# A two-block transformer kernel on one core: block 2's input projection and the query projection fed with unnormalised, turned residuals

## The reference, cut to what matters

```
x   = rms_norm(x2, norm_final)                      # end of the first block
h   = rms_norm(x, norm1_w) * (1 + scale1) + shift1  # scale, shift from silu(c) @ w_ada + b_ada
q, k, v, r, a_lr, su, sv, g_a, g_b = split(h @ w_in)
...                                                 # gated linear attention, spatial gating, merge
x   = x + gate1 * (merged @ w_out)                  # called x3 below
h2  = rms_norm(x, norm2_w) * (1 + scale2) + shift2
x   = x + gate2 * peer(h2)                          # queries h2 @ w_q, keys, top 16, experts
out = rms_norm(x, final_norm_w)
```

## Time and profile before

| what | value |
|---|---|
| median of 3 runs | 1415.91 us (1415.56 to 1416.72) |
| the profiled execution's own time | 1417.08 us |
| its span | 1415.3 us |
| granted TensorE clock, mean share of full | 0.988 |
| PE busy | 1371.8 us, 97% |
| POOL, DVE, ACT busy | 1055.6, 757.9, 710.4 us |

### The profile page before, as it was taken

One profiled execution on the slowest core, in us unless ns is written; L12 is line 12 of the kernel. 1 busy time (PEld: TensorE's weight loads), 2 busy tenths in 40 slices (PEclk: granted clock), 3 DMA queues, 4 the chain that ended last, 5 costly groups with the idle time before them and its releaser, 6 DMA issues.

```text
span 1415.3 us, 28961 instructions
## 1 busy us (share of the span) xinstructions
PE 1371.8 (97%) x9764; PEld 1220.6 (86%) x9764; DVE 757.9 (54%) x1617; ACT 710.4 (50%) x1133; POOL 1055.6 (75%) x469
## 2 busy tenths in 40 slices
PE   7998999999999998999999999999999999999997
PEld 7887899998877876999999999999977777878885
DVE  4655433335258526249991276666588788511113
ACT  6354555555355444435556533433455555556663
POOL 6654688886777985768888877777777777788885
PEclk9999999998999999999999999999999999999999
DMA  8453677763645456545555544444445444465552
GB/s 306 153 179 120 237 282 275 284 256 134 208 144 175 159 185 250 191 132 187 180 183 186 179 164 157 154 162 155 156 159 166 164 163 163 168 248 193 193 193 89
DMA packets 72651, 263.02 MB, mean 186 GB/s; under 512 B 8208, under 2 KB 9104, under 8 KB 72224
## 3 DMA queue, kind: packets, MB, share of 16 engines
q1 hardware_dynamic: 72608, 262.46, 53.9%
HBM read 259.81 MB, written 2.62 MB: 185 GB/s over the span
## 4 chain that ended last, share of the span: by engine, by line
PE 88%; DVE 6%; issue 2%; ACT 1%; DMA 1%; POOL 1%; SPq 0%; ACTq 0%; POOLq 0%; DVEq 0%
PE bank L865 14%; PE bank L883 14%; PE bank L866 14%; PE bank L867 14%; PE bank L884 13%; PE bank L885 13%; PE bank L1271 3%; DVE arena L1741 1%; POOL wlo L433 1%; DMA raw<-stream 1%; PE bank L983 1%; PE bank L1253 1%; DMA col<-cols 0%; PE bank L941 0%; DVE bank L1369 0%
## 5 line engine op out<-in xcount | busy, mean ns | idle before, releaser
L433 POOL TENSOR_TENSOR wlo<-raw,whi 128x1024 fp32r<-128x1024 f32 x432 | 1041.6, 2423 | 320.1 <-ACT whi L503 316.9
L503 ACT ACTIVATE whi<-raw 128x1024 fp32r<-128x1024 f32 x432 | 455.8, 1057 | 347.4 <-PE bank L885 256.9
L865 PE MATMUL bank<-xh,whi 128*128 128x256 f32 x1600 | 462.4, 289 | 4.2 <-DVE xl L1332 2.4
L866 PE MATMUL bank<-xl,whi 128*128 128x256 f32 x1600 | 455.4, 285 | 0.0
L867 PE MATMUL bank<-xh,wlo 128*128 128x256 f32 x1600 | 455.0, 284 | 0.0
L883 PE MATMUL bank<-whi,xh 128*128 128x512 f32 x800 | 321.6, 402 | 12.0 <-DVE xl L1939 4.1
L865 PEld LDWEIGHTS bank<-xh,whi 128*128 128x128 f32 x1600 | 309.8, 194 | 9.4 <-POOL wlo L433 3.7
L884 PE MATMUL bank<-wlo,xh 128*128 128x512 f32 x800 | 313.1, 391 | 0.0
L885 PE MATMUL bank<-whi,xl 128*128 128x512 f32 x800 | 312.9, 391 | 0.0
L866 PEld LDWEIGHTS bank<-xl,whi 128*128 128x128 f32 x1600 | 309.9, 194 | 1.2
L867 PEld LDWEIGHTS bank<-xh,wlo 128*128 128x128 f32 x1600 | 309.6, 193 | 0.0
(11 more groups left out here) (285 smaller groups left out, 1160.3 us busy)
## 6 DMA issues: line engine op xcount, KB each, us to landing
raw<-stream SPq DMA_DIRECT2D x432, 512.0 KB, 3.3
arena<-ada SPq DMA_DIRECT2D x48, 512.0 KB, 4.8
arena<-rows SPq DMA_DIRECT2D x5, 512.0 KB, 8.6
xs<-x SPq DMA_DIRECT2D x2, 512.0 KB, 6.0
arena<-rows SPq DMA_DIRECT2D x1, 1024.0 KB, 5.5
x_spill<-xs SPq DMA_DIRECT2D x1, 1024.0 KB, 6.1
xs<-x_spill SPq DMA_DIRECT2D x1, 1024.0 KB, 6.1
out<-arena SPq DMA_DIRECT2D x2, 512.0 KB, 2.6
```

The costliest lines, as they stand in the source:

```text
L433: nc.gpsimd.tensor_tensor(wlo[:, slot, :], raw[:, slot, :], whi[:, slot, :].bitcast(F32), ALU.subtract).then_inc(lo_done, 1)
L503: nc.scalar.activation(whi[:, slot, :], raw[:, slot, :], ACT.Copy).then_inc(hi_done, 1)
L865: nc.tensor.matmul(dst, h_, xh[:, k, :], start=(k == 0), stop=False)
L866: nc.tensor.matmul(dst, h_, xl[:, k, :], start=False, stop=False)
```

## The change

Both projections are fed from the raw residual: PE turns x2 (and x3) as soon as each 128x512 piece is there (`turn_of`), ACT and DVE apply only the gain (`upper_raw`, `turned_raw`), and the first tiles start without a norm. The activations get two more columns holding the shift (`xhs`, `xls`), so each of these f_tiles has 258 columns. The norm's root is turned into a row (`root_row`) after 3 (2) tiles, copied to `in2_r` (`wq_r`), and each tile's result is multiplied by the row and gets its own shift column added when it is read (`normed`, three DVE instructions in place of one). What follows needs the true h: DVE multiplies the turned banks by gain and row (`rowed`), ACT adds the shift (`shifted`), and at the end of the projection `xh` and `xl` are written anew (`upper_normed`, `turned_normed`). The two roots of block 2's input become one formula. `ada_columns` 3 to 7 move into the MLP, after 51 of its 64 tiles; the decays move into `m_sv`. `ada_row` 8 to 11 move between the projections' tiles, with new banks. SP's order changes with it: 12 tiles instead of 8 before block 2's constants, 16 instead of 8 query tiles before the spill, keys loaded before it. The last four tiles are done two banks at a time.

```diff
+            def turn_of(group, src, ready, tt, bs):
+                for b in bs:
+                    pe.wait_ge(S(ready), 2 * tt + b // 2 + 1)
...
+            def normed(n, d_, src, row, scale, done):
+
+                if n >= 2:
+                    v.wait_ge(S(done), n - 1)
+                wshift = wshifts[:, n % 2:n % 2 + 1]
+                own(nc.vector.tensor_copy(wshift, src[:, T:T + 1]))
+                own(ttt(d_, src[:, 0:T], row, ALU.mult)); own.sync()
+                if scale is None:
+                    tsc(d_, d_, wshift, None, ALU.add).then_inc(S(done), 1)
+                else:
+                    tsc(d_, d_, wshift, scale, ALU.add, ALU.mult).then_inc(S(done), 1)
...
+            def shift_lower(n, shifts):
+
+                v.wait_ge(S("shift_hi"), n)
+                ttt(xls[:, :, T:T + 2], shifts.unsqueeze(2).to_broadcast([P, KC, 2]), xhs[:, :, T:T + 2].bitcast(F32),
+                    ALU.subtract)
...
+                if i == N_FFN - 2:
+                    v.wait_ge(S("ada_cols"), 8)
+                    ttt(mod[:, :], bank[7][:, 0:32], c_("bada"), ALU.add).then_inc(S("mod_done"), 1)
...
+            def weighted(b):
+                v.wait_ge(S("x2_done"), b + 1)
+                ttt(xn[:, b // 2, (b % 2) * 512:(b % 2 + 1) * 512], x_half(b), tmp[:, (b % 2) * 512:(b % 2 + 1) * 512],
+                    ALU.mult).then_inc(S("x2_weighted"), 1)
...
+            shift_lower(SHIFTS["in2"], mod[:, 0:8])
+            weighted(0)
+            turned_raw("in2", gain_fin, (0, 1))
+            weighted(1)
+            turned_raw("in2", gain_fin, (2, 3))
+            weighted(2)
+            weighted(3)
...
+            for n in range(N_IN2_F):
                 v.wait_ge(tile_used, T_IN2_F + n + 1)
+                normed(n, qk[:, n, :], bank[IN2_BANK[n]], in2_r, 128 ** -0.5 if n < 4 else None, "qk_out")
+                if 2 <= n < 6:
+                    rowed("in2_T", gain_fin, in2_r, n - 2)
+                if n == 5:
+                    v.wait_ge(S("roots"), rooted("fin"))
+                    for tt in range(TT):
+                        stt(xres[:, tt, :], xres[:, tt, :], rs("fin", tt), tmp, ALU.mult, ALU.mult)\
+                            .then_inc(S("fin_done"), 1)
+                if n in (4, 6):
+                    gate_row(8 + (n - 4) // 2, gate1, "gate1_b").then_inc(S("gate1_done"), 1)
+            turned_normed("in2_T", "in2n")
...
+            def qk2_tile(n, turned=None, half=None):
+
+                pe.wait_ge(S("x2_done" if n < 3 else "qk_out"), n + 1 if n < 3 else n - 2)
+                f_tile((T_IN2_F + n) % R, T_IN2_F + n + 1, bank[IN2_BANK[n]][:, 0:T + 2], turned, xhs, xls, half)
+
+            for n in range(3):
+                qk2_tile(n, None if n else "in2")
+            pe.wait_ge(S("roots"), rooted("in2"))
+            pe.wait_ge(S("x2_done"), 4)
+            root_row("n1", bank[3], "in2_row")
+            qk2_tile(3)
+            pe.wait_ge(S("in2_row_out"), 1)
             ada_row(8)
+            qk2_tile(4)
+            qk2_tile(5)
+            pe.wait_ge(S("gate1_done"), 1)
             ada_row(9)
+            qk2_tile(6)
             pe.wait_ge(S("gate1_done"), 2)
+            qk2_tile(7, half="in2_half")
...
-            for b in range(4):
+            for banks in ((0, 1), (2, 3)):
                 for c in range(N_PEER - R, N_PEER):
-                    expert_m(c, None, final=(c == N_PEER - 1), banks=(b,), used=b == 3)
+                    expert_m(c, None, final=(c == N_PEER - 1), banks=banks, used=banks == (2, 3))
```

More of the change, by code:

```diff
@@ L394, in _ @@
                 ada_tile(n)
-            for n in range(T_WQ, T_WQ + 8):
+            for n in range(T_WQ, T_WQ + 16):
                 tile(n % R, n * P, n - R + 1)
@@ L867, in f_tile @@
                     last = nc.tensor.matmul(dst, l_, xh[:, k, :], start=False, stop=(k == KC - 1))
+                    if half and k == KC // 2 - 1:
+                        last.then_inc(S(half), 1)
                 last.then_inc(tile_used, 1)
@@ L1017, in ada_row @@
                 pe.wait_ge(ada_used, 4 * (g - g % 2 + 2))
-                nc.tensor.matmul(bank[6 + g % 2][:, :], one.to_broadcast([P, P]), ada_sum(g), start=True, stop=True)\
+                nc.tensor.matmul(bank[ROW_BANK[g]][:, :], one.to_broadcast([P, P]), ada_sum(g), start=True, stop=True)\
                     .then_inc(S("ada_rows"), 1)
@@ L1145, in _, with pairs @@
             transposes("mlp_T", "mlp", xres)
-            def pairs(base, count, group, name, name_of_turn):
+            LATE = 12
+            def pairs(base, count, group, name, name_of_turn, late):
                 def m_of(slot, count_, u, ready, **kw):
@@ L1175, in _ @@
-            for n in range(2, N_IN2_F):
-                pe.wait_ge(S("qk_out"), n - 1)
-                f_tile((T_IN2_F + n) % R, T_IN2_F + n + 1, bank[4 + n % 2][:, 0:T])
-            pe.wait_ge(S("gate1_done"), 2)
-            pe.wait_ge(S("xg_out"), 4)
-            pe.wait_ge(S("consts2_in"), 96)
-            for k in range(KC):
-                last = nc.tensor.matmul(bank[6][0:16, 0:T], wal[:, k, :], xg[:, k, :], start=(k == 0),
-                                        stop=(k == KC - 1))
@@ L1185, in _, with decays @@
-            last.then_inc(S("alr"), 1)
-            m_group(T_IN2_M, "m_sv")
+            qk2_tile(6)
+            pe.wait_ge(S("gate1_done"), 2)
+            qk2_tile(7, half="in2_half")
+            def decays(k):
+                if k != KC - 2:
+                    return
+                pe.wait_ge(S("xg_out"), 4)
+                pe.wait_ge(S("consts2_in"), 96)
+                for k in range(KC):
+                    last = nc.tensor.matmul(bank[6][0:16, 0:T], wal[:, k, :], xg[:, k, :], start=(k == 0),
+                                            stop=(k == KC - 1))
+                last.then_inc(S("alr"), 1)
@@ L1187, in _ @@
+            m_group(T_IN2_M, "m_sv", "in2n", before=decays)
             pe.wait_ge(S("alr_out"), 1)
```

336 lines of the change are left out of this document (201 added, 135 removed).

## The result

The changed kernel took 1436.88 us in the median of 4 runs (1436.01 to 1439.85), the one before 1416.32 beside it: a ratio of 1.0149, 95% interval 1.0133 to 1.0165. It is 1.5% slower, 8 us more than the 1428.9 of the forecast and above its range. The profiled execution took 1436.01 us (span 1434.1) against 1417.08, so 18.9 us are to be found.

A forecast was written before the change was run, and what follows sets the result against it. PE, busy 97% of the span, was taken as the bound, so only work put on it and holes in it count: 6.2 + 5.6 + 1.7 - 0.5 = +13.0 on the median 1415.91 gives 1428.9 us; range 1415.5 to 1433.5.

The forecast's parts named there:

- The columns, +6.2: In the full MLP, 40 matmuls cost all 4.5 us and a half-clock stretch 1.7; bounds 4.5 to 7.9.
- From the MLP to m_sv, +5.6: MLP's last matmul to m_sv: 46.9 us with DVE meeting POOL, against 41.3 before.
- The wait ahead of `ada_row(9)`: Projection: PE waits 2.5 us (0 to 2.6) for `gate_row(8)`, as meetings with `wlo` put DVE a tile behind.
- From wout2 to the scores, +1.7: wout2's last tile to the scores: 60.7 us against 59.0 before; with no meeting 56.4, so -2.6.
- The "nothing" for the steady tiles: Queries: `normed`'s tensor_scalar comes about in POOL's 0.48 us gap in each 2.88, so no cost.
- The tail, -0.5: Last tiles: pairs of banks cover PE's waits, but DVE sets the path; bank 1 comes 0.5 us earlier.
- seven f_tiles take 20.16 us, so one takes 2.88; I use 2.90 for 258 columns: Rebuilt projections: two more columns lengthen each f_tile by 0.02 us.
- The rival of the clock: PE's new waits of 3 to 4 us bring two or three clock falls: +4.5 us, 1433.4; chance 0.10.
- the forecast's own mechanism: Rebuilt stages: DVE instructions between SBUF operands meet POOL's `wlo` and last until it ends; forecast chance 0.40.
- The first rival: Rebuilt stages: DVE's instructions fall into POOL's gaps, so no meetings cost time: +0.1 us, 1416.0; chance 0.15.
- One reading of POOL: Kernel before: slow DVE rows lay under POOL's `wlo` of 2.40 us and lasted until it ended.
- its own test: Experts: if these stages, alike in both kernels, differ in length, the cause lies outside the forecast's steps.

The follow-up runs named there:

- b_cols: Kernel before with only the 40 one-column matmuls moved into the MLP; 1425.14 us, ratio 1.0074.
- a_psum: Changed kernel with the product of `normed` left in PSUM and the shift added from there; 1427.57 us, ratio 1.0091.
- b_tail: Kernel before with only the last tiles read by two banks at a time; 1416.53 us, ratio 1.0005.
- b_stride: Kernel before with only `xh` and `xl` made slices of tensors of 258 elements for each k; 1420.18 us, ratio 1.0031.
- a_layout: Changed kernel with residuals and arena at multiples of 1024 bytes, stride 258 only for the raw stages; 1432.63 us, ratio 1.0126.
- a_shift: Changed kernel with the shift columns written before the MLP's last read-outs; 1435.71 us, ratio 1.0143.
- b_xl64: Kernel before with `xl` moved to 64 bytes behind a multiple of 1024; 1417.76 us, ratio 1.0009.
- b_best: Kernel before in the aligned layout, stride 258 for f_tile in queries, experts and MLP, tail by two banks; 1408.24 us, ratio 0.9947.
- b_f258: Kernel before in the aligned layout, stride 258 for f_tile in the queries and experts; 1409.65 us, ratio 0.9954.
- b_shift: Kernel before with stride 256 kept and 64 unused bytes behind each of `xh` and `xl`; 1419.38 us, ratio 1.0027.

## Why the prediction was wrong

The direction was right, the size was not: +13.0 forecast, +21 measured. In the traces the miss is 5.9 us (18.9 against 13.0). By the starts on PE, +3.4 of it lies in the experts, +2.2 in the m tiles between m_sv and wout2's end beyond the decays, +2.0 between wout2 and the scores, less 1.6 up to the MLP's end, where before's trace has the half clock of 151.49:158.31 and the change's has not, and 0.2 from there to m_sv. By its steps:

- **The columns, +6.2:** right in the traces. 6.1 in the change, 6.0 alone in b_cols; 4.52 of work and one stretch of 3.4 us at half clock, as put. The times of b_cols say 9.6, and what the other 3 us are is open.
- **From the MLP to m_sv, +5.6:** right in the sum, 43.1 + 3.6 = 46.7 us against 46.9. The start took 5.4 (5.8), tiles 0 to 2 10.4 (10.0), the row 2.7 (3.0), tile 7 and the rewrite 6.2 (4.65), where the half clock came on top. The wait ahead of `ada_row(9)` (2.5) did not occur: DVE met POOL in `normed` 0, 1 and 6, but not in 3 and 4. This miss and that at tile 7 cancel for the most part, so the sum owes something to luck.
- **From wout2 to the scores, +1.7:** too small. From wout2's last matmul, 62.7 us against 60.7: tile 0 took 4.4 instead of 3.8, tiles 2 and 3 took 7.4 instead of 5.8, with the half clock of 589.19:592.60 on them, and 2.5 instead of 1.2 passed between the last tile and the scores. The start was 1.4 shorter than forecast, the first row sized right (3.9 against 4.0). The "nothing" for the steady tiles was wrong: `normed` met POOL in five of them, the last three among them, and the very last meeting stands ahead of the scores. By the table, whose tile 180 lies behind the scores, the stage costs 4.8, and a_psum takes 4.3 of it away.
- **The tail, -0.5:** right, in the traces of b_tail and of the change; no time can show it.
- **The step that failed** is "seven f_tiles take 20.16 us, so one takes 2.88; I use 2.90 for 258 columns". For those tiles it holds (2.87 us each in the queries). But it counted only what the wider slice adds to the two stages that use it, and nothing for what it does to every other matmul that reads the residuals: a new stride, and new addresses for all that is allocated behind. That was 4.4 us by b_stride's ratio from the one side, and 4.3 by a_layout's median from the other, with the pace in the experts going from 443 to 433 matmuls in 100 us and back. The change shows these lines, and the forecast gave them no term and no rival.
- **The rival of the clock** (two or three falls behind the new waits, 1.7 us each) was given one chance in ten and happened beside the forecast's own mechanism, not in its place. There were five, of which the ones at tile 7 and at query tiles 2 and 3 stand on steps that came out 1.6 us too long each. Put together, 1433.4 from that rival and 4.4 for the layout give 1437.8. That is close to what was measured, but it is a sum made after the result, and part of the queries' miss is POOL's and not the clock's.
- **The first rival** (DVE falls into POOL's gaps) fell: 0.86 us in the mean for `normed`'s last step (L1501) against 0.35 free of POOL. Its sum was also off: by the forecast's own bullets the projection without meetings comes to 39.3 us, not 38.3, and the queries' stage to 56.7, not 56.4, which makes the rival 1417.3 instead of 1416.0. In a_shift the wait moved to the next instruction between SBUF tensors. The Trainium skill (SBUF — State Buffer, Who interferes with whom) calls the shared port pair an exclusive lock. By that rule the next such instruction waits for the POOL instruction that is under way, and the trace agrees (0.68 us became 2.61).
- **One reading of POOL** was loose: the slow DVE rows did not all end with the `wlo` over them. The 2.50 us at L1880 ended 0.16 behind it, but each 3.30 at L1735 ended 1.1 behind, so DVE first waited and then did its own work, and the `wlo`s around it took 3.37 us instead of 2.40, so POOL too seems to have waited for DVE.
- The forecast named its own test: "If the expert stages, alike in both, differ in length, the cause lies outside these steps." They did, by -3.2 and +6.5 us, and that part of the cause did.

## What to carry to other kernels

When a change resizes or re-strides an on-chip tensor, ask which matmuls read it or anything allocated behind it, and compare their number in a window where PE is full, before looking at the stages that were meant to change. A full engine's pace is as much a part of the time as its waits: 2% on m_tile weighed about as much as a stage that was rebuilt. On DVE beside a busy POOL, let the short steps that others wait for take an operand from PSUM; in a_shift, moving one of them away only handed its wait to the next.

## What the runs showed of the hardware that was not expected

- The pace of m_tile goes with the start address of its stationary operands: 226.7 ns on a multiple of 1024 bytes, 231.1 when one of the two (`xl`) lies 64 bytes behind one. Most of the loss sits at one matmul: in b_xl64 those with `xh` take 228 to 229 ns to the next start, those with `xl` 236. That is not the whole rule: in b_best's MLP the matmuls with `ul` take 234.2 ns instead of b_f258's 227.6, with `ul` at the same address; in the MLP the two kernels differ in nothing but the stride of `xh` and `xl`.
- For the streamed operand it is the reverse: with 256 columns 120.0 ns from aligned tensors, 117.9 with the stride of 258 (b_f258), 117.8 with `xl` 64 bytes off (b_xl64), but 120.0 again when `xl` is 64 bytes off and all behind it moved by 128 (b_shift). And b_shift's own f_tiles take 117.7 in the MLP, from the same tensors. What decides, the addresses that PE reads or those that ScalarE and DVE use at the same time, is open. The Trainium skill (SBUF — State Buffer, Who interferes with whom) has it that on the engines' side only the port pair shared by VectorE and GpSimd contends and TensorE never waits; these runs neither prove nor refute that, but they show that the place of its operands is not free.
- Half-clock stretches came and went between traces of kernels that are alike there: one of 3.41 us at 1019 to 1040 us, behind PE's wait between the experts' halves, in the change and five of the twelve experiments; one of 3.41 or 6.83 us at 151 in before and six of them. Each moves a single trace by some 2 us.
